# A chunked linear recurrence in chunks of 32 tokens instead of 64

## The reference, cut to what matters

```
def step(S, inp):                       # one token, one head of 64 channels, S is 64 x 64
    r_t, w_t, k_t, v_t, a_t, b_t = inp
    sa = S a_t
    S  = S * w_t + sa b_t^T + v_t k_t^T
    y  = S r_t
...
mean = mean(y over the head); var = mean((y - mean)^2)
y = (y - mean) * rsqrt(var + LNX_EPS) * ln_g + ln_b
```

## Time and profile before

| | us |
|---|---|
| median of 3 runs (lowest, highest) | 1453.22 (1451.27, 1460.05) |
| the profiled execution | 1457.06 |
| its span from first to last instruction | 1455.3 |
| the eight trips, first transpose at 67.47, gate of the last trip at 580.10 | 513 |
| PE busy in the span | 1225.2 |

### The profile page before, as it was taken

The page is one execution under the profiler, slowest core; times in us unless marked ns, Lnnn a source line. Parts: engine busy times, 40 slices in busy tenths (PEclk is TensorE's granted clock), DMA queues, the critical chain, the costliest instruction groups (busy, mean ns, idle before and its releaser), DMA issues.

```text
span 1455.3 us, 27859 instructions
## 1 busy us (share of the span) xinstructions
PE 1225.2 (84%) x11826; PEld 708.2 (49%) x11826; DVE 519.1 (36%) x919; ACT 388.4 (27%) x735; POOL 249.2 (17%) x250
## 2 busy tenths in 40 slices
PE   5988999999999979996998787499928959988881
PEld 2455666576666657453554443244303445544440
DVE  6723343433343342223111110479982241111114
ACT  3323333323233321220111111345534211111112
POOL 2000000000000000041222111068860232221110
PEclk9999999999999989996999999799959979999996
DMA  6133010101001051338999998532700089999984
GB/s 149 44 6 49 3 49 2 49 5 47 22 29 49 2 212 53 106 143 340 419 421 421 423 421 316 231 87 58 274 0 19 29 329 415 420 421 423 422 364 197
DMA packets 149115, 271.85 MB, mean 187 GB/s; under 512 B 62178, under 2 KB 106210, under 8 KB 131584
## 3 DMA queue, kind: packets, MB, share of 16 engines
q1 hardware_dynamic: 136960, 240.68, 43.8%
q0 software_dynamic: 10880, 21.00, 3.8%
q10 hardware_dynamic: 1152, 8.39, 1.4%
HBM read 263.73 MB, written 23.07 MB: 197 GB/s over the span
## 4 chain that ended last, share of the span: by engine, by line
PE 62%; DMA 15%; DVE 8%; SPq 5%; POOL 4%; issue 3%; ACT 3%; POOLq 0%; DVEq 0%; ACTq 0%
PE psum L1198 12%; DMA big<-in_moe_w_up_dram 10%; PE psum L1378 10%; PE psum L807 10%; PE psum L1660 8%; POOL big L1862 4%; PE psum L820 4%; SPq L352 2%; DVE psum L1964 2%; PE psum L1882 2%; DMA conv_w<-in_moe_w_up_dram 2%; PE psum L1355 2%; DVE h L911 1%; PE psum L1334 1%; SPq L353 1%
## 5 line engine op out<-in xcount | busy, mean ns | idle before, releaser
L807 PE MATMUL psum<-big 128*64 128x256 f32 x1728 | 225.9, 407 | 43.4 <-DMA big<-in_moe_w_up_dram 29.5
L1198 PE MATMUL psum<-big 128*128 128x512 f32 x384 | 186.9, 613 | 6.5 <-ACT big L1232 3.8
L807 PEld LDWEIGHTS psum<-big 128*64 128x64 f32 x1728 | 124.2, 145 | 130.6 <-DMA big<-in_moe_w_up_dram 41.3
L1378 PEld LDWEIGHTS psum<-big 64*64 64x64 f32 x4096 | 137.3, 136 | 46.8 <-issue 46.8
L1378 PE MATMUL psum<-big 64*64 64x64 f32 (+1 forms) x4096 | 146.9, 227 | 5.3 <-issue 2.1
L721 POOL TENSOR_SCALAR big<-big 128x1024 f32<-128x1024 f32 x8 | 22.8, 2851 | 700.6 <-PE psum L460 700.5
L882 DVE TENSOR_TENSOR big<-big,psum 128x128 f32<-128x128 f32 x64 | 18.4, 288 | 332.5 <-ACT big L848 332.5
L1517 ACT COPY big<-psum 128x512 f32<-128x512 f32 (+1 forms) x104 | 62.3, 623 | 255.8 <-PE psum L1378 159.5
L749 POOL DMA_INDIRECT chosen<-big x64 | 63.8, 997 | 352.4 <-PE psum L786 139.7
L1660 PE MATMUL psum<-big 128*128 128x512 f32 x256 | 116.8, 609 | 6.0 <-ACT big L1934 5.6
L820 PE MATMUL psum<-big 128*64 128x512 f32 x512 | 120.8, 592 | 1.2 <-ACT big L853 1.2
(11 more groups left out here) (250 smaller groups left out, 1519.3 us busy)
## 6 DMA issues: line engine op xcount, KB each, us to landing
big<-in_moe_w_down_dram SPq DMA_DIRECT2D x64, 1024.0 KB, 23.6
big<-in_moe_w_gate_dram SPq DMA_DIRECT2D x54, 1024.0 KB
big<-in_moe_w_up_dram SPq DMA_DIRECT2D x54, 1024.0 KB
big<-in_rwkv_w_rkv_dram SPq DMA_DIRECT2D x24, 512.0 KB, 4.9
conv_w<-in_moe_w_gate_dram SPq DMA_DIRECT2D x10, 1024.0 KB
conv_w<-in_moe_w_up_dram SPq DMA_DIRECT2D x10, 1024.0 KB
conv_w<-in_conv_w_pw_dram SPq DMA_DIRECT2D x16, 512.0 KB, 5.2
big<-chosen ACTq DMA_DIRECT2D x8, 1024.0 KB, 8.1
```

The source lines that it names most:

```text
L807: last = nc.tensor.matmul(o[half * SLOTS:(half + 1) * SLOTS, 0:F_EXP].rearrange("p (u f) -> p u f", u=2), m.xT[e // 2 % 2][:, c, (e % 2) * ...
L1198: last = nc.tensor.matmul(bank[b], m.w[:, n, c, :], x[:, c, :], start=(c == 0), stop=(c == C - 1))
L1378: last = nc.tensor.matmul(o[half(par), at:at + w.shape[1]], lhs(hd, cp, par), w, start=True, stop=True)
```

## The change

The chunk is 32 tokens long. There are 16 chunks, four of them beside each other on the partitions (`quarter(par)`, 32 partitions each). Every stage of `blocks` and `product` then has 32 small products instead of 16, each on a 32-row or 32-column part of the array; walks over `units` go through the four quarters in turn, and the new `crossed` alternates the head with the quarter. The join of the 16-token blocks needs one factor less: the stages mt, m2 and wz go away, and x1's result plus dr is already the answer (`wz`). The state products keep 64 columns; the output products have 32.

The sums for state and output are cut in two halves of quarters, (0, 1) and (2, 3), that write the same PSUM columns one after the other. The projection of v is cut in 16 half pieces (128x256): two stand between the output sums, fourteen in the loop, after chunks 0 to 13. K's pieces stand as 6 and 2 instead of 4 and 4, r's as 2, 1, 1, 2, 2.

The values v are centred over the head before they enter the recurrence (DVE: `tensor_reduce` and `scalar_tensor_tensor` in place of ACT's copy of vt), so y has mean zero; the mean product L1313 and the subtraction L1561 go away, and ACT squares y at the start of the next trip.

```diff
-        CH = 64
+        CH = 32
...
-        CP = NCH // 2
+        NQ = P // CH
+        CP = NCH // NQ
...
-            for hd in range(2):
-                for cp in range(CP):
-                    for par in range(2):
+            for cp in range(CP):
+                for hd in range(2):
+                    for par in range(NQ):
                         yield hd, cp, par
+
+        CROSSED = tuple(((par + hd) % 2, par) for hd in range(2) for par in range(NQ))
+
+        def crossed(pars):
+
+            for cp in range(CP):
+                for hd, par in CROSSED:
+                    if par in pars:
+                        yield hd, cp, par
...
+        def pe_prepare_v_part(m, pe, q, step):
+            c, part = step // 2, step % 2
...
+            cols = slice(part * (T // 2), (part + 1) * (T // 2))
+            last = nc.tensor.matmul(bank[1][:, cols], m.w[:, 2, c, :], m.xv[:, c, cols], start=(step == 0),
+                                    stop=(c == C - 1), skip_group_check=True)
...
-                for hd, cp, par in units():
-                    c = slice((2 * cp + par) * CH, (2 * cp + par + 1) * CH)
-                    last = nc.tensor.matmul(bank[b + hd][half(par), lo_ + cp * CH:lo_ + (cp + 1) * CH],
-                                            lhs[half(hd), c], rhs[half(hd), c], start=True, stop=True)
+                for hd, cp, par in crossed(range(NQ)):
+                    c = slice((NQ * cp + par) * CH, (NQ * cp + par + 1) * CH)
+                    last = nc.tensor.matmul(bank[b + hd][quarter(par), lo_ + cp * CH:lo_ + (cp + 1) * CH], lhs[half(hd), c],
+                                            rhs[half(hd), c], start=True, stop=True)
...
-            blocks(mat(m.lo_), mat(m.dt), 5).then_inc(m.mm_ps.now(), 1)
-            blocks(mat(m.dt), mat(m.lo_), 6).then_inc(m.mt_ps.now(), 1)
-
-            wait(m.lv_ready)
-            blocks(mat(m.dt), tok(m.att), 2, n=2 * CH)
-            blocks(mat(m.dt), mat(m.lv), 2, n=2 * CH, lo_=CH).then_inc(m.dr_ps.now(), 1)
-            wait(m.mm_ready, m.mt_ready)
-            blocks(mat(m.mt), mat(m.mm), 7).then_inc(m.m2_ps.now(), 1)
...
+            blocks(mat(m.lo_), mat(m.dt), 5).then_inc(m.mm_ps.now(), 1)
+            blocks(mat(m.dt), tok(m.att), 6, n=HD, wide=2 * HD)
+            blocks(mat(m.dt), mat(m.lv), 6, n=HD, wide=2 * HD, lo_=HD).then_inc(m.dr_ps.now(), 1)
...
+            wait(m.mm_ready, m.dr_ready)
+            blocks(mat(m.mm), mat(m.dr), 2, n=2 * HD, wide=2 * HD).then_inc(m.x1_ps.now(), 1)
...
+            decayed((0, 1))
+            state_sums((0, 1)).then_inc(m.first_sums_ps.now(), 1)
...
+            wait(m.first_sums_ps)
+            decayed((2, 3)).then_inc(m.rg_ps.now(), 1)
+            state_sums((2, 3))
+            wait(m.rh_ready)
+            output_sums((0, 1)).then_inc(m.first_y_ps.now(), 1)
+            if more:
+                pe_prepare_v_part(m, pe, nq, 0)
+            wait(m.first_y_ps)
+            output_sums((2, 3)).then_inc(m.z_ps.now(), 1)
+            if more:
+                pe_prepare_v_part(m, pe, nq, 1)
...
-                if more and c < 4:
-                    pe_prepare_v(m, pe, nq, 4 + c, 5 + c)
+                if more and c + 2 < 2 * C:
+                    pe_prepare_v_part(m, pe, nq, c + 2)
...
+            w(m.vt_ps)
+            values = bank[2].rearrange("p (u i) -> p u i", i=HD)
+            nc.vector.tensor_reduce(m.vsum, values, AX.X, ALU.add).then_inc(m.vsum_ready.now(), 1)
+            w(m.vsum_ready)
+            STT(out=m.vt.rearrange("p c (h i) -> p (c h) i", i=HD), in0=m.vsum.unsqueeze(2).broadcast_to([P, 2 * CP, HD]),
+                scalar=-1.0 / HD, in1=values, op0=ALU.mult, op1=ALU.add).then_inc(m.vt_ready.now(), 1)
```

More of the change, by code:

```diff
@@ L1054, in pool_rwkv_masks @@
             for half in range(2):
-                p = slice(half * CH, half * CH + CH)
+                p = slice(half * HD, half * HD + HD)
                 step(nc.gpsimd.memset(m.heads[p, half * HD:half * HD + HD], 1.0))
+                step(sel(out=m.eye64[p, :], in_=ones[p, 0:HD], compare_op=ALU.is_equal, fill=0.0, base=0, pattern=[[-1, HD]],
+                         channel_multiplier=1))
                 step(nc.gpsimd.memset(m.head_mean[p, half * HD:half * HD + HD], 1.0 / HD))
+            for quarter in range(NQ):
+                p = slice(quarter * CH, quarter * CH + CH)
                 one = ones[p, 0:CH]
@@ L1308, in dve_prepare_rest @@
                 op1=ALU.mult).then_inc(m.rk_ready.now(), 1)
-        def pe_moment_mean(m, pe, p, b):
-            pe_wait(pe, m.y_ready.sem, m.y_ready.by(p))
-            nc.tensor.matmul(bank[b], m.head_mean, m.y, start=True, stop=True).then_inc(m.mean_ps.now(), 1)
         def pe_moment_var(m, pe, p, b):
@@ L1396, in pe_rwkv_pair @@
             blocks(mat(m.u2), mat(m.l2), 6).then_inc(m.l4_ps.now(), 1)
[L1397 removed]
+            blocks(mat(m.lak), tok(m.vt), 7, n=HD).then_inc(m.lv_ps.now(), 1)
             if more:
@@ L1439, in pe_rwkv_pair @@
-            wait(m.m2_ready, m.x1_ready)
-            blocks(mat(m.m2), mat(m.x1), 6, n=2 * CH).then_inc(m.wz_ps.now(), 1)
-            if more:
-                pe_prepare_v(m, pe, nq, 2, 4)
-            else:
-                mix_first(1, 6, PAIRS - 1)
-            wait(m.wz_ready)
-            for hd, cp, par in units():
-                w = m.wz[half(par), hd, cp, 0:CH]
-                nc.tensor.matmul(bank[2 + par][half(hd), cp * CH:(cp + 1) * CH], w, m.mrb[half(par), hd, cp, :],
-                                 start=True, stop=True)
-                last = nc.tensor.matmul(bank[2 + par][half(hd), 256 + cp * CH:256 + (cp + 1) * CH], w,
-                                        m.btt[half(par), cp, hd * HD:(hd + 1) * HD], start=True, stop=True)
@@ L1468, in pe_rwkv_pair, with add_to @@
-            last.then_inc(m.z_ps.now(), 1)
+                mix_first(1, 5, PAIRS - 1)
+            wait(m.wz_ready)
+            def add_to(pars, b, lo_, n, lhs, rhs, start, stop):
+                for hd, cp, par in crossed(pars):
+                    c = NQ * cp + par
+                    at = lo_ + (c // 2) * n
+                    last = nc.tensor.matmul(bank[b + c % 2][half(hd), at:at + n], lhs(hd, cp, par), rhs(hd, cp, par),
+                                            start=start or (start is None and c < 2), stop=stop, skip_group_check=True)
+                return last
```

209 lines of the change are left out of this document (101 added, 108 removed).

## The result

The changed kernel takes **1644.18 us** (median of 4 runs, 1638.16 to 1661.12) against 1454.09 (4 runs) of the kernel before on the same chip: a ratio of **1.132**, 95% interval 1.127 to 1.136. The forecast was 1519 in a range of 1460 to 1595: the direction was right, the size far out. The profiled execution took 1644.15 us.

A forecast was written before the change was run, and what follows sets the result against it. PE bounds the recurrence, and after the change its instruction feed sets the middle. 1457.1 + 40 (six trips) - 3.6 (vanished wait) + 20 (first trip) + 10 (last) = 1523 profiled, 3.8 above the median: 1519 us, range 1460 to 1595.

The forecast's parts named there:

- Counting: Per trip 1660 small MATMUL records instead of 924, about 3550 instructions or 13.9 blocks; about 143 packets on q8 overall.
- One sign named ahead: Sign of being right: small-product stretches average never under 28 ns over 128 records, though runs inside them are.
- Head: Start of each trip, without the mean product: 4.8 us instead of 5.7.
- The second trip's wait for a low-rank weight: PE's 3.61 us wait at 141.29, behind table loads on SP, vanishes because PE comes later: -3.6 us.
- Middle: Trip between head and loop: set by the instruction feed at 50.0 us (47.4 to 54.9), from 49.05; 42.2 without the feed.
- Loop: End of each trip, fourteen PE-bound half-piece steps at 1.0 us: 15.6 us (14.2 to 17.0) where 9.0 stood, +6.6.
- rival C: Feed-bound, plus clock drops in stalls or small records at 20 to 25 ns: trips 75 to 80 us, total 1570; chance 0.13.
- A step that isn't at 1.0: Sign of being wrong: loop steps with a half piece of v not taking 1.0 us each.
- First trip: Table loads fill the DMA engines, so six more instruction blocks come late: +20 us, bounds +8 and +30.
- Last trip: Expert weights fill the engines and more instruction blocks fall into that window: +10 us, bounds +5 and +20.
- A (feed hidden): Instruction feed hidden in the trips: trip 62.6 us or less, total 1387 to 1444, centred on 1415; chance 0.14.
- B: Small products on array parts don't overlap beyond two: trip 86.1 us, +22.3, total 1630; chance 0.13.

## Why the prediction was wrong

- **Counting** held: 142 packets for 143; many bursts between stalls are one block long. (The kernel before has sixteen calls of `blocks`, not thirteen as told above; its 512 records were counted right.) One sign named ahead did not hold: stretches of 128 small records were never to average under 28 ns, but 164 in a row took 1.98 us, 12 ns each. And a sum was off: the low end of a trip, 4.8 + 47.4 + 14.2 = 66.4, is +2.6 and not +3.6, which puts the forecast's own low end at 1478 instead of 1484.
- **Head**: 4.8 forecast, 4.87 at full clock. Most heads were entered at 1.2 GHz and took 6.3 to 7.0, one 11.4 with a feed stall of 2.8 us. So the heads too missed by what the clock cost. The second trip's wait for a low-rank weight went, as forecast.
- **Middle**: 50.0 forecast, 52.1 to 54.4 measured. The middle at 539.30 has six stalls for instructions, 10.1 us together, and 52.68 - 10.1 = 42.6 without them: the work was forecast at 42.2, the stalls at 7.8. The other middles have a mean clock of 0.88 to 0.96 besides. With half the products the stalls went down to 2.0 us or less, so they hang on the instructions.
- **Loop, the step that failed**: 15.6 was priced at full clock; the one loop at full clock took 15.4, the others 25.9 to 28.4. The text saw the fall of the clock after a stall in the last trip, and again the stalls that it forecast, but kept the two apart: a fall was given 0.13 as part of rival C, with trips of 75 to 80 us. Stalls were forecast in every trip, so the fall had to be in the forecast itself, and its price worked out: fourteen steps bound by PE at half the clock, 14 x 0.74 = 10.4 us. The trips took 75 to 89 us. A step that isn't at 1.0 was named ahead as a sign of being wrong, and it was the one that showed: 1.72.
- **First trip**: +20 forecast, +46 measured, over the bound of +30; its middle took 27.0 us more than before, 22 of them gone when the table loads are moved away, and its loop, at 1.2 GHz, 19.3 more.
- **Last trip**: +10 forecast, +23 measured, over its bound of +20; 7.6 in the middle and 15.5 in the loop (26.3 us, at 1.2 GHz).
- **Rivals**: A (feed hidden) is out by 8 to 11 us of stalls in the middle of each of six trips, and more in the first and the last. By the Trainium skill (Runtime: NRT & Kernel Launch, Instruction fetch mechanics) crossing a block is mostly hidden; dense small products show the contrary, in every trip (7.7 us of stalls in the middle and more). B is out: small records pass at 10 to 12 ns, in four row parts that write one bank. That B's total, 1630, lies nearest to the 1644 measured is chance: it had 65.7 for the middle and full clock in the loop. C named the fall of the clock, and sized it too small.
- The Trainium skill (TensorE: Matmul & The Clock Gate, A second HAM failure mode: psum-queue depth-cycling) tells of a bf16 kernel in which short idle stretches between groups of matmuls make the clock go up and down. The trace of the changed kernel agrees: each of the seven falls that a loop inherits stands beside a stall for instructions, of 0.5 to 1.4 us, or of 3.9 in the first trip, and at most some 2 us behind its end.

What is shown: the loop holds full clock if it is entered with it and PE doesn't run dry in it (at 591.98, and four times with half the products), costs 10.5 us more if it is entered at 1.2 GHz, and gets it back with more large work in it or ahead of it. What is argued from the places of the falls: that the stalls for instructions bring the clock down. The clock also fell behind short waits for other engines, with no such stall near (three cases above), and which stall suffices is open: before the loop at 591.98 one of 0.59 us left the clock at full, before the loop at 666.50 one of 0.51 us was followed by a fall. The rival that the sums' small products by themselves do it was not tested apart from the stalls, as leaving half of them out changes both. Nor was the full 32-token kernel run without its stalls: its instructions can't be made fewer without leaving out work.

## What to carry to other kernels

Count the instructions of a stretch against what the feed delivers (here 256 in 3.8 to 4.2 us) before making matmuls smaller; in a dense stretch what the array saves below that is lost again at the next block. Where a stall is forecast, price the PE-bound work behind it at 1.2 GHz as well. And try the order of small matmuls over the quarters of the array before their size: it gave 3.5 us a trip at no cost.

## What was not expected of the hardware

- Added useless matmuls made the kernel 19 us faster (a 128x256 product in each loop step), because they brought the clock back.
- 64x64 records go at 29.5 ns when two quarters on the diagonal alternate and at 20.5 when two column halves of the same rows do, at 34 when neighbours share a part, and at 14.7 when all four quarters take turns.
- One load of 4-byte elements (15.5 KB) made a middle that is bound by the feed 4 to 9 us longer, and two of them made one 17 us longer, with stalls of 8.6 and 8.4 us.
